# Reordering six expert-weight loads in SyncE's queue ahead of the first gather of a hierarchical MoE layer

## The reference

```python
mix = jnp.concatenate([attn, conv], axis=-1) @ w_out[l]
x = _layer_norm(DEEPNORM_ALPHA * x + gate1 * mix, ln1_g[l], ln1_b[l])
h2 = (x * (1.0 + scale2) + shift2).reshape(bsz * seq, d)
# router: top-1 of 4 groups, top-2 of the 8 experts in it -> combine weights
for g in range(N_GROUPS):        # 32 experts: 1024 -> 256 (gate, up) -> 1024 (down)
    hid = jax.nn.silu(jnp.einsum('td,edf->tef', h, w_gate[g])) \
        * jnp.einsum('td,edf->tef', h, w_up[g])
    y = y + jnp.einsum('tef,te,efd->td', hid, combine[:, g], w_down[g])
x = _layer_norm(DEEPNORM_ALPHA * x + gate2 * moe, ln2_g[l], ln2_b[l])
```

## Time and profile before

| what | value |
|---|---|
| time, median of 3 runs | 546.74 us (546.0 to 547.13) |
| time of the profiled execution | 545.14 us |
| its span, first to last instruction | 543.3 us, so 1.84 us lie around it |
| TensorE matmul busy | 505.3 us (93%) |
| VectorE busy | 285.2 us (52%) |
| mean granted TensorE clock | 0.979 |
| bytes moved by DMA | 169.22 MB, of these 152.22 on SyncE's queue |

### The profile page before, as it was taken

The page is one execution under the profiler, slowest core; times in us unless marked ns, Lnnn a source line. Parts: engine busy times, 40 slices in busy tenths (PEclk is TensorE's granted clock), DMA queues, the critical chain, the costliest instruction groups (busy, mean ns, idle before and its releaser), DMA issues.

```text
span 543.3 us, 6459 instructions
## 1 busy us (share of the span) xinstructions
PE 505.3 (93%) x2504; PEld 272.2 (50%) x2504; DVE 285.2 (52%) x520; ACT 99.9 (18%) x164; POOL 127.4 (23%) x119
## 2 busy tenths in 40 slices
PE   3999999999999999999997999999998899898983
PEld 2455468744444444444683555555554455454531
DVE  4774999763937293365888622322222222222488
ACT  1000211233223230000342111111120111121130
POOL 2000000065378350241533011111110012110016
PEclk9999999999999999999997999999998899989997
DMA  9999779954640244999587999999999999999763
GB/s 264 356 360 353 231 237 316 302 213 155 228 153 7 78 139 183 352 419 387 195 289 301 412 410 416 417 414 417 417 416 417 414 415 417 419 413 416 311 242 154
DMA packets 71280, 169.22 MB, mean 311 GB/s; under 512 B 7902, under 2 KB 45842, under 8 KB 63056
## 3 DMA queue, kind: packets, MB, share of 16 engines
q1 hardware_dynamic: 64304, 152.22, 74.2%
q0 software_dynamic: 4464, 8.12, 4.0%
q10 hardware_dynamic: 2480, 8.44, 3.9%
HBM read 159.60 MB, written 17.30 MB: 326 GB/s over the span
## 4 chain that ended last, share of the span: by engine, by line
PE 61%; DVE 14%; DMA 11%; SPq 9%; issue 3%; ACT 1%; POOL 0%; DVEq 0%; POOLq 0%; ACTq 0%
PE ps L1612 17%; PE ps L1490 11%; PE ps L1532 10%; PE ps L1621 9%; DVE acc_part L933 5%; SPq L415 4%; DMA w_gu<-in_w_up_dram 4%; PE ps L1602 3%; PE ps L1460 3%; DMA ada_stage<-in_w_ada_dram 2%; DMA w_stage<-in_w_in_dram 2%; PE ps L1479 2%; DMA y_tok<-y_dram 2%; DMA y_dram<-ysb,slot_row 1%; SPq L420 1%
## 5 line engine op out<-in xcount | busy, mean ns | idle before, releaser
L1612 PE MATMUL ps<-w_gu,xT 128*64 128x256 f32 x1024 | 120.1, 388 | 3.4 <-issue 1.6
L1612 PEld LDWEIGHTS ps<-w_gu,xT 128*64 128x64 f32 x1024 | 72.4, 139 | 41.1 <-issue 4.1
L1490 PE MATMUL ps<-hT,w_stage 128*128 128x512 f32 x192 | 84.8, 595 | 0.0
L1254 DVE TENSOR_TENSOR ysb<-ps,rows_gate 64x512 f32<-64x512 f32 x64 | 44.1, 689 | 60.4 <-PE ps L1621 59.9
L1621 PE MATMUL ps<-w_dn,hidT 128*64 128x512 f32 x256 | 63.4, 617 | 5.9 <-issue 4.3
L1245 DVE TENSOR_TENSOR hid<-ps,silu_sb 128x128 f32<-128x128 f32 x32 | 9.3, 291 | 93.2 <-ACT silu_sb L844 93.2
L933 DVE SCALAR_TENSOR_TENSOR acc_part<-ada_stage,csil,acc_part 128x256 f32<-128x256 f32 x112 | 55.2, 493 | 4.0
L1490 PEld LDWEIGHTS ps<-hT,w_stage 128*128 128x128 f32 x192 | 35.5, 190 | 41.0 <-issue 41.0
L1532 PE MATMUL ps<-wo,mixT 128*128 128x512 f32 (+1 forms) x144 | 55.6, 546 | 0.0
L641 POOL DMA_INDIRECT y_dram<-ysb,slot_row x15 | 15.1, 1007 | 150.3 <-DVE ysb L1254 150.3
L1401 PE MATMUL ps<-hT,w_first 128*128 128x512 f32 x96 | 44.5, 609 | 0.9 <-DVE hT L959 0.9
(11 more groups left out here) (210 smaller groups left out, 514.2 us busy)
## 6 DMA issues: line engine op xcount, KB each, us to landing
w_gu<-in_w_gate_dram SPq DMA_DIRECT2D x32, 1024.0 KB, 19.6
w_gu<-in_w_up_dram SPq DMA_DIRECT2D x32, 1024.0 KB, 22.8
w_dn<-in_w_down_dram SPq DMA_DIRECT2D x32, 1024.0 KB, 24.9
ada_stage<-in_w_ada_dram SPq DMA_DIRECT2D x16, 1024.0 KB, 7.7
w_stage<-in_w_in_dram SPq DMA_DIRECT2D x9, 1024.0 KB, 9.9
ada_in<-in_w_ada_dram SPq DMA_DIRECT2D x12, 512.0 KB, 9.5
y_dram<-zeros ACTq DMA_DIRECT2D x4, 1024.0 KB, 6.2
wo<-in_w_out_dram SPq DMA_DIRECT2D x2, 2048.0 KB, 11.4
```

The lines of the kernel that those rows point to most:

```text
L1254: ins = w.tensor_tensor(to[e * HD:(e + 1) * HD, b * 512:(b + 1) * 512], ps[b * HD:(b + 1) * HD, down_bank(y), :], gate2r[b * HD:(b + 1) * ...
L1490: ins = t.matmul(ps[:, 6], st[:, k, (f % 2) * P:(f % 2 + 1) * P], hT[:, k], start=k == 0, stop=k == KC - 1)
L1612: ins = t.matmul(ps[a * SLOTS:(a + 1) * SLOTS, GATE_BANK[e], 0:2 * P], rows_in[:, k, e * SLOTS:(e + 1) * SLOTS], weights[:, :, k, a * P:(a ...
```

## The change

The SP loads ahead of the first reuse of a ring are put in another order, and the two halves of expert 5 get separate waits. No other engine's program is touched, and the same 22 blocks are loaded.

```diff
             sp.wait_ge(out_done, TC + 2)
             load_gu_part(6, 0)
+            for i in (0, 1):
+                sp.wait_ge(st_x1[i], 16)
+            load_gu_part(GU_RING - 1, 0)
             sp.wait_ge(out_done, NOUT)
             load_dn(4)
             load_gu_part(6, 1)
-            for i in (0, 1):
-                sp.wait_ge(st_x1[i], 16)
-            load_gu_part(GU_RING - 1, 0)
+            sp.wait_ge(logit_done, TC - 1)
+            load_gu_part(5, 0)
             sp.wait_ge(logit_done, TC)
-            load_gu(5)
-            sp.wait_ge(x1_last, 2 + 2 * len(X1_BY_DVE))
-            load_gu_part(GU_RING - 1, 1)
+            load_gu_part(5, 1)
             for n in range(2):
                 sp.wait_ge(st_h2[n], 32)
             load_dn(5)
+            sp.wait_ge(x1_last, 2 + 2 * len(X1_BY_DVE))
+            load_gu_part(GU_RING - 1, 1)
             load_gu(GU_RING)
```

## The result

The changed kernel is slower: 548.17 us (median of 13 runs, 547.0 to 549.29) against 546.55 us (13 runs, 545.46 to 547.61), ratio 1.0031, 95% interval 1.0022 to 1.0040, so 1.2 to 2.2 us. The prediction had 546.1, with a range up to 547.9. The profiled execution was 547.0 us with a span of 545.2; it is the fastest of the 13, so the profile shows the changed kernel at its best.

A forecast was written before the change was run, and what follows sets the result against it. The prediction took an unbroken stream of weights from about 297 us on to bound the kernel. A gain of 0.9 us less 0.3 for gather 0 gave 0.6: 546.74 − 0.6 = 546.1 us, range 545.0 to 547.9.

The forecast's parts named there:

- the lid: Expert 8's gate half, the 23rd block, can't be issued before TensorE frees buffer 0 at 300.82; nothing moves that forward.
- the 19 stretches: Stretches of 10 us from 300 to 490 us, in the expert half: DMA engines always busy, at 413 to 417 GB/s.
- gather 0 queues behind `w_dn5`: Rival ahead of the experts: late down block still queued when gather 0 comes; at full 3.4 us, 549.2; chance 0.15.
- The dips: Low DMA rates in 276 to 278 and 284 to 286; filling them with earlier gate halves wins at most 1.2 us.
- over 350 GB/s from 276 to 293: Sign of a right forecast: the DMA rate expected in the new profile ahead of the expert half.
- The end of the stream ahead of the gather: Weight stream ahead of gather 0 runs dry at 293.3: 292.0 plus 2.5 for the down block, less 1.2 won.
- The price of the tail: Delay of gather 0 by the last block's tail, an overlap of some 0.3 to 0.5 us; taken as 0.3 us.
- the two bounds, 0 and 3.4: Bounds on gather 0's delay: none, or the 3.4 us by which gather 1, made while blocks were queued, took longer.
- The rule that I set against the row: DMA engines alternate queues by packet, so 0.5 us overlap costs gather 0 at most about 0.25; gather 1's row disagreed.
- The gain: Expert 8's gate half, issued into a drained queue at 300.82, lands at 305.5 instead of 306.4: 0.9 us gained.
- the low bound that I had, 0.1: Low end of the gain at expert 8's gate half, 0.1 us, if it lands after 5.5 us as `w_dn4` did.
- The fit of 4.4 us: Skill's price for a 1 MB transfer, 2.0 us plus bytes at 436 GB/s; gain would be 1.2 us; not used.

The follow-up runs named there:

- the third edit alone: The kernel before with only the down block of buffer 5 moved ahead of the x1_last wait; ratio 1.0044, median 548.72 us.

## Why the prediction was wrong

The place, the bound and the path were right: the stream of weights sets the end, expert 8's load is the lid, gather 0 is on the path to it. (Two small slips change nothing: the 19 stretches run from 411 to 420 GB/s, and expert 8's load is issued 0.05 us after the modelled end of expert 0's matmuls, 297.10 + 3.67 = 300.77, and not "to the hundredth".) The price of the gather was wrong, and with it the sign of the sum. The result is the rival that I called "gather 0 queues behind `w_dn5`", with a chance of 0.15, but at 1.8 us and not at its full 3.4. Of the signs named for a wrong forecast the first came: a wait of TensorE much longer than 0.61 us, and expert 8 issued after 301.7. The measured 548.17 lies above the range, which ended at 547.9. Step by step:

**The dips.** "0.5 MB or 1.2 us of stream" won by the first two edits was nothing. From 274 to 290 us the rate is the same; this is the row of the kernel before, to set against the one above:

```profile
274.00:290.00 16.00, 11.50 (x101) 10.35 (x100) 13.71 (x58) 6.06 (x8) 2.59 (x3) 0.94 0.91 339
```

Both moved 339 GB/s over these 16 us. The dip at 284 to 286 did fill (410 GB/s instead of 332), but 278 to 280 fell from 332 to 295, and the gate half issued at 274.71 did not have the stream at rate before 277 (106 GB/s in 276 to 277). So the sign "over 350 GB/s from 276 to 293" did not come either: it was 242 in 276 to 278 and 295 in 278 to 280.

**The end of the stream ahead of the gather.** "It runs dry at 293.3" was about 1.5 us too early. The stream moved 0.29 MB in 294 to 295 and 0.06 in 295 to 296. This follows from the step before: without the 1.2 us won, and with this trace 0.25 us late, the sum is 292.0 + 2.5 + 0.25 = 294.75.

**The price of the tail.** "I take 0.3 us, near the low end, since only the tail of the last block is in the way." This is the step that failed most: it measured 1.8 us. I had the two bounds, 0 and 3.4, and chose by a picture of the overlap. The overlap itself was not 0.3 to 0.5 us but about 1.4, from 293.7, where the gather's packets were due, to 295.1. In its first 0.6 us the gather got no packet; then both queues moved, and a few last packets made it later still (17 packets of q0 in 294 to 295, against 121 in 294 to 295 before). The rule that I set against the row, the Trainium skill's round of the queues (DMA: Bandwidth & Descriptors, on queues, rings and completion order), would have cost half of the overlap, 0.7 us by this estimate for 1.4 us; the trace here does not agree with a price so small, and the measurement decides.

Neither bound had the order of the change. Gather 1, the bound of 3.4, had two blocks issued behind it (295.04 and 295.45 against its own start at 294.59); gather 0 of the changed kernel had one block issued 1.9 us ahead of it.

**The gain.** 0.9 us was worked out from a landing (4.7 us in a drained queue). What the stream feels is when it is at rate again, and that is 2.1 us after the issue: 172 GB/s in 304 to 305 and 426 in 305 to 306 after the issue at 302.90. Before, the queue's backlog reached just as far, in this row of the kernel before:

```profile
300.00:305.00 5.00, 4.20 (x39) 2.54 (x37) 3.35 (x13) 0.54 (x2) 0.00 (x0) 1.00 1.05 422
```

So the low bound that I had, 0.1, was the nearer one. As for the landing itself, 4.7 us was a good choice: where expert 8's gate half went into a drained queue and its landing is listed, it took 4.8 to 4.9 us. The fit of 4.4 us that stands beside the sum is given by the Trainium skill (DMA: Bandwidth & Descriptors, on the anatomy of one DMA) for transfers that GpSimd issues, and this block is SyncE's.

With 0 for the gain and 1.8 for the gather the sum is +1.8 us, 548.3 against the median before at 546.55, and 548.17 was measured. That it fits so well is partly luck: the third edit alone, with the same release, came out 2.2 us slower.

**Not thought of.** The clock: in one of three profiles of the changed kernel the wait on the gather (2.58 us) was followed by matmuls at half clock.

## What to carry to other kernels

A load moved up into idle DMA time is free only as long as its bytes are through when the next transfer that an engine waits for has its first packets due. Here that was 2.0 us after the gather's instruction started: a stream that ended by then cost nothing, one that ran 0.6 us longer cost 1.8. Count that end from the last observed one plus the bytes added, without bytes that earlier loads are only hoped to win. When a release of a buffer caps the prefetch, filling a hole ahead of it gains nothing if the queue already reaches over the restart. Where two bounds are far apart and no row has the order of the change, neither bound's size carries over, and the forecast has to hold both.

## What the runs showed of the hardware

A gather of GpSimd issued while one 1 MB block more of SP's was queued ahead landed after 5.4 to 6.0 us, against 4.1 to 4.3 where the queue ran dry within 2.0 us of the start of its instruction; with half that block it was 4.1. Alone its first packets came 2.0 us after that start, in the changed kernel 2.6. After a drained queue SP's stream was at full rate only some 2 us after the issue. And nearly the same wait of TensorE, 2.52 and 2.58 us, left its clock at full in one execution and was followed by 0.58 (mean over 2 us) in another.
